# Grid attention stage: gate product z inside it, decays on another engine, score products in pairs of 64-row tiles

## The reference

```
p = h @ w_in                                     # q, k, v, gate z, xs, B, C, step sizes
attn = neighbourhood_attention(q, k, v, kc, vc, rpb, rows)     # 8 heads of 64, softmax over 256 + 256 keys
y_f, h_f = ssd_chunked(xs, dt[..., 0, :], a[0], bm, cm, h0_fwd)
y_b, h_b = ssd_chunked(flip(xs), flip(dt[..., 1, :]), a[1], flip(bm), flip(cm), h0_bwd)
y = y_f + flip(y_b) + d_skip[:, None] * xs
y = y.reshape(bsz, l, SSD_WIDTH) * jax.nn.silu(z)
x = x + g1 * (jnp.concatenate([attn, y_ssd], axis=-1) @ w_out)
```

## Time and profile before

| | us |
|---|---|
| median of three runs | 1012.01 |
| lowest, highest | 1011.74, 1013.97 |
| the profiled execution | 1013.08 |
| its span, first to last instruction | 1011.2 |
| stretch of the z products | 683.75 to 694.60 |
| grid stage: first score product to the first product of the output projection | 718.87 to 783.52 |

### The profile page before, as it was taken

One profiled execution on the slowest core, in us unless ns is written; L12 is line 12 of the kernel. 1 busy time (PEld: TensorE's weight loads), 2 busy tenths in 40 slices (PEclk: granted clock), 3 DMA queues, 4 the chain that ended last, 5 costly groups with the idle time before them and its releaser, 6 DMA issues. The chain is left out here.

```text
span 1011.2 us, 14855 instructions
## 1 busy us (share of the span) xinstructions
PE 978.2 (97%) x5836; PEld 836.7 (83%) x5836; DVE 696.0 (69%) x997; ACT 511.3 (51%) x686; POOL 55.2 (5%) x73
## 2 busy tenths in 40 slices
PE   7989999999999999999999999999998989999997
PEld 4568899988978877899998987888865779999996
DVE  2576658999755665657778565456688587777775
ACT  2465565445446655544445563554444354444443
POOL 0210000000001200000001010000010000000000
PEclk9999999999999999999999999999999999999999
DMA  9122566767756633668887552234101336555541
GB/s 364 61 98 98 216 255 219 280 227 270 260 189 213 225 118 120 225 242 329 297 326 290 197 220 94 92 130 144 42 1 42 130 141 213 183 181 184 183 178 42
DMA packets 28943, 185.05 MB, mean 183 GB/s; under 512 B 3680, under 2 KB 4384, under 8 KB 9312
## 3 DMA queue, kind: packets, MB, share of 16 engines
q1 hardware_dynamic: 23472, 155.54, 42.6%
q0 software_dynamic: 4416, 28.31, 7.5%
q10 hardware_dynamic: 1008, 0.55, 0.2%
HBM read 181.76 MB, written 2.62 MB: 182 GB/s over the span
## 5 line engine op out<-in xcount | busy, mean ns | idle before, releaser
L1950 DVE TENSOR_TENSOR split<-raw,split 128x2048 fp32r<-128x2048 f32 x122 | 279.6, 2292 | 179.7 <-ACT split L1414 178.2
L1414 ACT ACTIVATE split<-raw 128x2048 fp32r<-128x2048 f32 x121 | 231.4, 1912 | 242.1 <-PE bank L710 224.9
L708 PE MATMUL bank<-acts,split 128*128 128x256 f32 (+1 forms) x960 | 278.5, 290 | 2.5 <-DVE acts L1990 1.4
L710 PE MATMUL bank<-acts,split 128*128 128x256 f32 (+1 forms) x960 | 276.7, 288 | 0.0
L709 PE MATMUL bank<-acts,split 128*128 128x256 f32 (+1 forms) x960 | 276.7, 288 | 0.0
L708 PE MATMUL bank<-split,acts 128*128 128x512 f32 (+1 forms) x544 | 211.1, 388 | 1.4 <-DVE split L1950 1.0
L709 PE MATMUL bank<-split,acts 128*128 128x512 f32 (+1 forms) x544 | 208.7, 384 | 0.0
L710 PE MATMUL bank<-split,acts 128*128 128x512 f32 (+1 forms) x544 | 208.6, 383 | 0.0
L708 PEld LDWEIGHTS bank<-acts,split 128*128 128x128 f32 x960 | 183.8, 191 | 10.0 <-issue 3.4
L709 PEld LDWEIGHTS bank<-acts,split 128*128 128x128 f32 x960 | 183.8, 191 | 3.6 <-issue 0.2
L710 PEld LDWEIGHTS bank<-acts,split 128*128 128x128 f32 x960 | 183.8, 191 | 1.9
(11 more groups left out here) (254 smaller groups left out, 1062.5 us busy)
## 6 DMA issues: line engine op xcount, KB each, us to landing
raw<-w_mlp SPq DMA_DIRECT2D x64, 1024.0 KB, 4.8
raw<-w_glu SPq DMA_DIRECT2D x22, 1024.0 KB, 4.8
bias<-w_ada POOLq DMA_DIRECT2D x14, 1024.0 KB, 6.7
raw<-w_qkv SPq DMA_DIRECT2D x12, 1024.0 KB, 5.1
arena<-w_glu_down SPq DMA_DIRECT2D x22, 512.0 KB, 3.3
work<-w_ada POOLq DMA_DIRECT2D x10, 1024.0 KB, 5.9
raw<-w_mla_o SPq DMA_DIRECT2D x4, 1024.0 KB, 5.1
raw<-w_moba_o SPq DMA_DIRECT2D x4, 1024.0 KB, 4.8
```

What stands on the lines that cost most here:

```text
L708: pe.matmul(out_, a[0], b[0], start=first, stop=False)
L710: return pe.matmul(out_, a[1], b[0], start=False, stop=last)
L1414: return act.activation(out_, in_, ACT.Copy)
L1950: v.tensor_tensor(split[:, c % 2, 1, 0:n], raw[:, c % 2, 0:n], split[:, c % 2, 0, 0:n].bitcast(F32), ALU.subtract).then_inc(lo_ready, 1)
```

## The change

1. The products of z move from ahead of k into steps 0 to 3 of the grid stage, a quarter each. The chunk order becomes q, k, z, out. ACT copies the two gate tiles out in steps 3 and 4 and activates both at once behind the loop; DVE applies the gate behind the loop.
2. The subtraction and clamp of the decays go from DVE to ACT, as a Relu of the negated value with the bias from `stat`; the exponential then has scale -1. The G product becomes one 512-column fp32r pass: the cumulative sums are kept as a rounded part in rows 0 to 7 and the rest in rows 32 to 39 of a new tile `cumr`, and a new `pick` tile selects both.
3. The zero-padded queries go. `nqT` is one tile, and the scores of both heads of a pair for one token tile are two matmuls on rows 0 to 63 and 64 to 127, into two banks. Steps are taken pair by pair: head 0 tile 0, head 1 tile 0, head 0 tile 1, head 1 tile 1 (`head_and_tokens`). DVE forms the logits two steps ahead instead of one.
4. The last keys are transposed into a small bank and all keys are in place before step 0; the tables that set the steps are new.

```diff
-         ("v", 2, 4, 2), ("xs", 2, 4, 1), ("bc", 2, 4, 1), ("q", 2, 2, 2), ("z", 2, 2, 2), ("k", 2, 6, 1),
+         ("v", 2, 4, 2), ("xs", 2, 4, 1), ("bc", 2, 4, 1), ("q", 2, 2, 2), ("k", 2, 6, 1), ("z", 2, 2, 2),
...
-DECAY = (1, 2, 4, 5, 7, 8, 10, 11)
-SEGMENTS = [("G", 0), ("G", 1), ("K", 1), ("F", 0), ("G", 2), ("G", 3), ("F", 1), ("G", 4), ("G", 5), ("F", 2), ("G", 6),
-            ("G", 7), ("F", 3)]
-SEGMENT_STEP = {("K", 1): 1, **{("G", h): DECAY[h] - 2 for h in range(1, H)}, **{("F", n): 3 * n + 1 for n in range(4)}}
+DECAY = (0, 1, 5, 6, 8, 9, 11, 12)
+CARRIED = (2, 3, 7, 10)
+SEGMENTS = [("G", 0), ("G", 1), ("F", 0), ("F", 1), ("G", 2), ("G", 3), ("F", 2), ("G", 4), ("G", 5), ("F", 3), ("G", 6), ("G", 7)]
+SEGMENT_STEP = {**{("G", h): DECAY[h] - 1 for h in range(1, H)}, **{("F", n): CARRIED[n] - 1 for n in range(4)}}
+MIXED = (4, 5, 7, 8, 10, 11, 13, 14)
+WEIGHTED = (3, 4, 7, 8, 11, 12, 15)
 
 
 def grid_order():
 
-    first = [("S", 0), ("S", 1), ("G", 0), ("S", 2)]
+    first = [("S", 0), ("G", 0), ("C", 1), ("K", 1)]
     steps = []
     for i in range(2 * H):
         steps.append(("P", i))
-        steps.extend(x for x in SEGMENTS if SEGMENT_STEP.get(x) == i)
-        if i + 3 < 2 * H:
-            steps.append(("S", i + 3))
-        if i - 1 in DECAY:
-            steps.append(("Y", DECAY.index(i - 1)))
-        if i % 2 == 0 and i:
-            steps.append(("O", i // 2 - 1))
+        if i % 2 == 0 and i + 2 < 2 * H:
+            steps.append(("S", i // 2 + 1))
+        if i < 4:
+            steps.append(("Z", i))
+        else:
+            steps.extend(x for x in SEGMENTS if x[0] == "G" and SEGMENT_STEP.get(x) == i)
+        if i in MIXED:
+            steps.append(("Y", MIXED.index(i)))
+        if i in WEIGHTED:
+            steps.append(("O", WEIGHTED.index(i)))
+        steps.extend(x for x in SEGMENTS if (x[0] == "F" or i < 4) and SEGMENT_STEP.get(x) == i)
     steps.append(("O", H - 1))
     units, n = {}, 0
     for kind, i in first + steps + [("T", 0), ("T", 1)]:
-        if kind in ("S", "P", "T"):
+        if kind == "S":
+            units[(kind, 2 * i)], units[(kind, 2 * i + 1)] = n, n + 1
+            n += 2
+        if kind in ("P", "T", "K"):
             units[(kind, i)] = n
             n += 1
     return first, steps, units
+
+
+def head_and_tokens(i):
+
+    return 2 * (i // 4) + i % 2, i // 2 % 2
...
-            rows_units(GC["z"], GU["z"], 4, 512, 512, both[:2], 2)
...
+            def gate_products(t, part_):
+
+                u = GU["z"] + t
+                if t == 0:
+                    weights_in(GC["z"] + part_)
+                if part_ == 0:
+                    gemm_start(u)
+                w = slot(GC["z"] + part_, 4, 512)
+                for k in range(4):
+                    ins = product(gbank(u)[:, :], both[t](4 * part_ + k), tuple(p[:, k, :] for p in w),
+                                  part_ == 0 and k == 0, part_ == 1 and k == 3)
+                if part_:
+                    ins.then_inc(gemm_ready, 1)
+                elif t:
+                    ins.then_inc(down_used, 1)
...
-                    u = window_unit(kind, i)
-                    h, t = i // 2, i % 2
-                    if i == 8:
-                        pe.wait_ge(seg_free, SEGMENTS.index(("K", 1)) + 1)
-                    small_start(u)
-                    pe.matmul(sbank(u)[:, :], nqT[h % 2][:, h // 2, t * P:(t + 1) * P], nkT[:, h // 2, :],
-                              start=True, stop=True).then_inc(small_ready, 1)
+                    p, t = i // 2, i % 2
+                    if i == 4:
+                        gemm_gone(pe, ku + 5)
+                        small_gone(pe, window_unit("K", 1))
+                    for e in range(2):
+                        small_start(window_unit(kind, 2 * i + e))
+                    for e in range(2):
+                        pe.matmul(sbank(window_unit(kind, 2 * i + e))[:, :], nqT[64 * e:64 * e + 64, p, t * P:(t + 1) * P],
+                                  nkT[64 * e:64 * e + 64, p, :], start=True, stop=True).then_inc(small_ready, 1)
...
-                    for d in range(2):
-                        ins = pe.matmul(seg_bank[:, d * T:(d + 1) * T], repeated(ident, 8 * d + i, P),
-                                        cum_rows[:, d * T:(d + 1) * T], start=True, stop=True)
-                    ins.then_inc(seg_ready, 1)
+                    if i == 0:
+                        pe.wait_ge(cum_parts, 1)
+                    pe.matmul(seg_bank[:, :], repeated(pick[:, :], i, P), cumr[:, :], start=True, stop=True)\
+                        .then_inc(seg_ready, 1)
...
-            used(GC["z"])
-            used(GC["z"] + 1)
-            for t in range(2):
-                u = GU["z"] + t
-                gemm_out(act, u)
-                act.activation(sz[:, t, :], gbank(u)[:, :], ACT.Silu).then_inc(gemm_free[u % 4], 1)
...
+            def decay(h):
+
+                segment_out(act, "G", h)
+                if h >= 2:
+                    act.wait_ge(w_mat, h - 1)
+                for n, (a, e, src, t) in enumerate(parts):
+                    c = 256 + 8 * t + h + 16 * (n // 2)
+                    ins = act.activation(E[h % 2][:, a:e], seg_bank[:, src:src + e - a], ACT.Relu, scale=-1.0,
+                                         bias=stat[:, c:c + 1])
+                ins.then_inc(seg_free, 1)
+                act.wait_ge(seg_free, SEGMENTS.index(("G", h)) + 1)
+                act.activation(E[h % 2], E[h % 2], ACT.Exp, scale=-1.0).then_inc(seg_exp, 1)
+
+            window_exp(0)
+            for i in range(2 * H):
                 if i == 1:
                     context_keys(1)
-                if i == 14:
-                    pair_out(2)
+                    pair_empty(window_unit("K", 1), pair(nkT, 1))
                 if i:
-                    h, t = (i - 1) // 2, (i - 1) % 2
-                    u = window_unit("P", i - 1)
-                    small_out(act, u)
-                    copy(view(att, 2048 + 1024 * (h % 2), 4, T)[:, :, t * P:(t + 1) * P], halves(u, 4, P))\
-                        .then_inc(small_free[u % 4], 1)
-                if i == 2:
-                    segment_out(act, "K", 1)
-                    copy(pair(nkT, 1), seg_bank[:, :].rearrange("p (a b) -> p a b", a=2)).then_inc(seg_free, 1)
-                if i in (6, 10):
+                    turned_out(i - 1)
+                if i == 3:
+                    gate_rows_out(0)
+                if i + 1 < 2 * H:
+                    window_exp(i + 1)
+                if i == 1:
+                    used(GC["k"] + 1)
+                if i == 4:
+                    gate_rows_out(1)
+                if i in (5, 9, 13):
                     pair_out(i // 4 - 1)
-                if i == 12:
-                    used(GC["k"] + 1)
+                if i in DECAY:
+                    decay(DECAY.index(i))
+                if i in (4, 7):
+                    used(GC["z"] + (i == 7))
+            turned_out(2 * H - 1)
+            for t in range(2):
+                gemm_gone(act, GU["z"] + t)
+            act.activation(sz, sz, ACT.Silu).then_inc(z_act, 1)
...
-            v.tensor_copy(cum, sbank(u)[0:16, :]).then_inc(small_free[u % 4], 1)
+            v.tensor_copy(cum[0:8], sbank(u)[0:8, :]).then_inc(small_free[u % 4], 1)
+            small_gone(v, u)
+            step(v.tensor_tensor(pick[:, :], ident[:, 0:8], ident[:, 32:40], ALU.add))
+            step(v.tensor_copy(cumr[0:8, :], cum[0:8]))
+            settle()
+            v.tensor_tensor(cumr[32:40, :], cum[0:8], cumr[0:8, :].bitcast(F32), ALU.subtract).then_inc(cum_parts, 1)
...
+            for i in range(2):
+                window_logits(i)
+            for i in range(2 * H):
+                window_normalise(i)
+                if i + 2 < 2 * H:
+                    window_logits(i + 2)
+                if i in CARRIED:
+                    carried_rows(CARRIED.index(i))
                 if i - 1 in DECAY:
                     matrix(DECAY.index(i - 1))
-                if i == 13:
+                if i == 1:
                     used(GC["k"] + 1)
-                if i == 14:
-                    gated_rows(0)
-                if i == 16:
-                    gated_rows(1)
-                if i in (6, 10, 15):
+                if i in (5, 8):
+                    used(GC["z"] + (i == 8))
+                if i in (5, 9, 13):
                     pair_lo(i // 4 - 1)
+            for t in range(2):
+                gated_rows(t)
```

150 lines of the change are left out of this document (64 added, 86 removed).

## The result

The changed kernel takes 1018.12 us (median of six runs, 1016.46 to 1020.82) against 1012.91 for the kernel before (six runs beside it). The ratio is 1.0053, with an interval of 1.0039 to 1.0067: it is slower by about 5 us, where 6 us less were forecast and 1011 was the upper end of the range. The profiled execution took 1016.46 us with a span of 1014.7, 3.4 us more than the profiled one of before; it is the fastest of the six, 1.7 us under their median.

What follows compares the result with a forecast made beforehand. TensorE bounds the stage, with DVE close behind. Moving z and the longer stage, -10.85 + (70 - 64.65) = -5.5, then 1013.08 - 5.5 - 1.07 = 1006.5 us; range 1000.5 to 1011.

Steps and rivals of the forecast that it cites:

- Moving z: Ahead of k: z's products leave, 10.85 us gained there, first score product at 708.0; inside the stage they cost the same.
- Score pairs: Grid stage, TensorE: two 64-row tiles fully overlap, 0.86 us a pair, saving 6.9; mode entry 0.15 per pair.
- The two rivals with partly or wholly serial pairs: Score pairs in the grid stage: partial overlap, 1.29 a pair, 1010 us, chance 0.1; serial, 1.72, 1015 us, chance 0.08.
- the sum of 60.7: Grid stage: TensorE's own work, 60.5 - 6.9 - 5.0 + 10.9 + 1.2 = 60.7 us.
- Decay product, decays on ACT: Grid stage: decay product as one 0.226 us pass, saving 5.0; four decay pieces on ACT 1.45, with exponential 2.3.
- The placement by hand: Grid stage, steps 0 to 15 placed by instruction times: waits mostly after step 4, 9 to 13 us, stage 70 us.
- Normalise at 0.6 everywhere: Grid stage, DVE: the hand placement took each normalise at 0.6 us.
- The clock: Grid stage, TensorE: work counted at the full granted clock seen before; no term for a lower clock.
- The sum 60.7 + 9.3 = 70: Grid stage: 60.7 us of TensorE work plus 9.3 of waits make 70 us, against 64.65 before.
- the slower one (1015): Score pairs: tiles run serially and the array drains at each mode change, 8.4 us dearer, 1015 us, chance 0.08.
- the smooth rival: Grid stage: waits no longer than the earlier 4.2 us, stage 63 to 65, kernel 1001 to 999.5 us, chance 0.2.
- T late: Behind the stage: with ACT 3 us later than placed, T waits 2 us, 1008.5 us, chance 0.04.

Runs made afterwards that it cites:

- the run with 128 rows: Both score products of a pair over all 128 rows, against the changed kernel with matrix and carried rows ahead of the logits on DVE: 1009.32 us, ratio 0.9962.
- The fillers: 41 short unused float32 products put into TensorE's waits, against the changed kernel: 1012.42 us, ratio 0.9992.
- the better order: Carried rows and matrix moved ahead of the logits on DVE, against the changed kernel: 1006.83 us, ratio 0.9936.
- the split late: Second split of out's chunk moved later, against the changed kernel with matrix and carried rows before logits and ACT's decay before `pair_out`: 1005.2 us, again 1005.27.

## Why the prediction was wrong

Point by point, by its own steps.

**Moving z: right.** The first score product came at 706.35, where 708.0 was forecast, but 1.5 us of that were there before z's place. From the transposes ahead of k to the first score product it is 24.77 us (681.58 to 706.35) where it was 35.60 (683.10 to 718.70), so 10.83 left; 10.85 was forecast. No k product lost its cover. Inside the stage, the z blocks keep steps 0 to 3 short of waits as placed, but for one that came out at 0.69 instead of 0.5 (transposes at 728.85). They take 2.8 to 2.9 us each, where 2.7 was put.

**Score pairs: side by side, as taken; the price of the mode too small.** The forecast was 0.86 and 0.15 per pair; the trace shows 1.06 by the starts, 0.1 more in the transposes ahead of it, and the run with 128 rows puts the saving at 0.55 instead of 0.71. The two rivals with partly or wholly serial pairs (1.29, 1.72) are out: the records of the two heads start 7 ns apart. This, the z blocks, the decay products and smaller things make the 61.8 to 62.3 us of work that the profiles at full clock show, 1.1 to 1.6 over the sum of 60.7.

**Decay product, decays on ACT: right in the main.** A decay product takes 0.34 us to the start of Y in place of 0.23, up to 0.9 us in eight; the four pieces take 1.35 us where 1.45 was taken, the exponential 0.84.

**The placement by hand: right in kind, late in size.** It gave P of step 7 at 38.3 us of the stage, measured 40.7; up to there it drifts by 0.3 us a step. It named the chain (logits ahead of the matrix, ahead of normalise) and TensorE's waits: 9 to 13 us, measured 12.14. For the segment bank it had 5.2, measured 3.3; for the transposes and the scores 7.4, measured 8.7. It took the order on DVE as given and never asked what a swap would bring, so it had no idea how much of these waits was that one order.

**Normalise at 0.6 everywhere: wrong.** Taking the decay off DVE and putting the logits further ahead removed what had stood between the matrix and the normalise. The matrix's end releases POOL, and the normalise begins with it: 0.98 instead of 0.49 in five steps, 2.8 us in all and some 2 of TensorE's waits. My working had no line for who else starts when the matrix ends. The earlier trace rows show the row of before in which the logits lie in that place, and they are not slowed.

**The clock: the step that failed.** The sum 60.7 + 9.3 = 70 added the waits to the work at full clock, as in the earlier trace rows; what the waits themselves do to the clock it put at nothing, without a reason. There TensorE's waits were 4.2 us in 64.65. With 12 us of waits, most of them between 739 and 783 and up to 2.01 at a time, the clock fell twice. From the 10.3 us by which the stage exceeded the forecast (80.33 to 70), 6.0 us are P, G, Y and O at 1.2 GHz, 1.5 the undersized work, and 2.8 more waits, about the size of the slow normalises. The fillers settle that the 6 us hang on the waits. With them the kernel took 1012.42 us, the time of before (ratio 0.9992) and still above the range of the forecast: the clock alone turned no gain into a loss, and the rest of the miss is waits and work. None of the rivals had this: the slower one (1015) was a serial mode change, which didn't occur; the 0.07 given to "slower" was right by its sign alone. One slip of the working changes nothing: a stage of 65 us by the smooth rival gives -10.5, not -10.85.

**T late: did not occur.** TensorE issues T at 794.40 without a wait, with DVE done with the scaling at 792.55.

**What stays open.** Why the very same program has a stretch at 1.2 GHz in one execution and none in the next; no run varied one wait alone. The decays on DVE with the better order were not run. Nor was it tried whether z's blocks placed later in the stage, in steps 5 to 14, would replace the fillers by useful work; its second weight chunk and ACT's split of it would have to move as well.

## What to carry to other kernels

Where work is taken off the bounding engine, ask what its waits do to its clock: 12 us of waits cost 6 us more here, and short products without use in the waits were worth 6 us in one kernel and, by four runs, 2.5 in another. In a hand-made order let an instruction that needs a far product stand behind those that are ready, however early it was meant to be; two moved lines turned +5 us into -6. And when an instruction is taken out from between two others, look at which engine the first of them releases, and what it shares with the second.

## What the runs showed of the hardware

- In the grid stage TensorE's clock fell from 2.4 to 1.2 GHz for 3.41 or 6.83 us at a time (once for 10.24, with the decays back on DVE), where TensorE was at work but had waits close together. In the changed kernel it fell at 747.3 behind one of 2.01 us, and at 767.7 in one of 1.80 us that followed one of 1.39; with the split late it fell once although no wait was over 0.9 us, and in other executions of that program it held. The Trainium skill (TensorE: Matmul & The Clock Gate, Part 1: The HAM clock gate) says that activity sets the share of clock pulses that are let through, which the kernel with fillers bears out (granted clock 1.00 through its whole stage).
- Products whose result nobody uses kept the clock up: 0.998 or 0.999 in all ten runs with 41 of them, against 0.988 to 0.992 without. A record of 128 columns of them takes 0.12 us (sixteen in 1.95 us in the filled kernel).
- A normalise on DVE, 128x512 in SBUF with a factor per row, takes 0.98 us instead of 0.49 if a POOL addition of 0.73 us starts 0.03 us before it, and 0.65 if it starts 0.36 before. The Trainium skill (SBUF — State Buffer, SBUF: two separate sides) says that the two engines share a port pair, and that whichever starts first, GpSimd or certain forms of DVE instruction, holds it for a whole instruction while the other is blocked. The rows agree but for 0.2 us: blocked to the end of POOL's record it would have been 1.19 and 0.86 us (the profile's spans on POOL are rough). Logits beside the same addition keep their 0.69; they start 0.16 us ahead of it and read a PSUM bank (743.16 and 743.32 before).
- Two float32 products of 512 columns on 64-row tiles start 7 ns apart and take 1.06 us to the next start (754.76 to 755.82), against 1.72 on 128 rows (twice 0.86, rows 3). Some 0.1 more falls on the transposes ahead.
